# The row of a head's cumulative decays made by one full-height fp32r product in place of a 32-row f32 product

## Chip, core and metric

One NeuronCore of a Trainium2 chip runs the whole program. The metric is the device time of one execution in microseconds. Engines: PE is TensorE, PEld its weight loads, DVE is VectorE, ACT is ScalarE, POOL is GpSimd; SPq issues the DMAs.

## What is computed

The program is three layers on 256 tokens of width 1024: a first block (a mixer with a convolution branch and an SSM branch, then a mixture of 64 experts) and two layers of a second kind. The change lies in the SSM branch of the first block's mixer. Cut to that:

```
dt = softplus(n @ w_in[:, 7168:7200] + dt_bias)          # 32 heads, 256 tokens
ad = dt * a;  a_cs = cumsum(ad) within a chunk           # a = -exp(a_log)
seg[l, s] = a_cs[l] - a_cs[s];  L = exp(seg where s <= l)
y_diag = ((C B^T) * L) @ (x * dt)                         # for each head
```

The kernel works with chunks of 128 tokens (two of them) and carries the second chunk's share of the first through `rest`, the decay from each token of the first chunk to that chunk's end. To form `seg` for a head, the cumulative decays of that head, one row of 256 numbers, must stand on all 128 partitions.

## The kernel before

Weights stream from HBM into four slots of a ring (SyncE, `mixer_sp`, list `LOADS`), each slot refilled when the product four places back in the list is done. PE (`mixer_pe`) does first the projections: blocks of 8 accumulating products of 128x128 by 128x256 in f32 (`group`, line 176), then the 32-column product of `dt` (line 385), two "fillers" (blocks of the gate and z projection, also line 176), and the transposes of `dt`, `cs` and `rest` (line 171). An f32 product is two MATMUL instructions and two weight loads in the trace; an fp32r product is one of each.

DVE (`mixer_ve`) makes `dt` (lines 722, 724), `ex` = -dt*exp(a_log) (725), the two scans that give `cs` (728), `rest` (729), and then copies the five transposed pieces out as `col` (731).

The loop over heads, 34 steps on each of PE, DVE and ACT, is written out in a fixed order. On PE a step h holds, in this order: `decay(h)` (line 431, the product that the change replaces); a filler unless h % 4 is 3; in every fourth step pieces of the modulation rows (lines 333, 342); at h = 5, 13, 21 `prepare` of the next group of eight heads (417, 418 and eight transposes, 171); `mix(h-2)` (lines 443, 444), and behind the last odd heads of a group a sum of squares (201). On DVE a step holds `decay(h)` (three subtractions from the product's bank, 753 to 755), `weigh(h-1)` (759), a few taps of the convolution (700), `prepare` (737 to 745), `mix(h-2)` (765, 768) and, at h = 10, 18, 26, `norm` (reciprocal 218, then 777). On ACT: the exponential of step h (583), the copy of a filler (568 or 570), a square (194), and at h = 10, 18, 26 the square root (208), each change of function with a table load.

PE takes one of seven PSUM banks for each product and waits till the engine that last read that bank is done (`Ring.take`), so that nearly each product group begins with a wait:

```
b = ring.take(("cs", h))
if h == 0:
    e.wait_ge(*k.at("col", 1))
e.matmul(k.pb[b][:, 0:T], ident[0:32, h:h+1] broadcast to [32, 128], m_.cs, ...)
```

`mix(h)` on PE waits for `weigh(h)` on DVE. Behind the loop stand the remaining fillers, the convolution's mean and the mixer's tail (lines 488 to 490: fp32r products of values split into a rounded part and a remainder), then the experts, whose weights stream for about 950 us, then the two layers.

Of the kernel before, what the change touches and what calls it, by code (L numbers as in the profile page):

```python
# [7 lines left out]
F32 = mybir.dt.float32  # L8
# [3 lines left out]
ALU = mybir.AluOpType  # L12
ACT = mybir.ActivationFunctionType
# [3 lines left out]
T = 256  # L17
# [17 lines left out]
for _l in range(2):  # L35
# [3 lines left out]
CONST = [("ident", 128), ("ones", 128), ("amask", 128), ("lmask", 128), ("before", 128), ("iota", 256), ("upto", 64),  # L39
         ("kthr", 8), ("shift", 1), ("m64", 64), ("first", 1), ("cos", 32), ("sin", 32)]  # L40
ROWS = [("brt", 72), ("qhg0", 96), ("khg0", 96), ("qhg1", 96), ("khg1", 96)]
# [230 lines left out]
def mixer_sp(k, e):  # L272
# [4 lines left out]
    for n, (what, i) in enumerate(LOADS):  # L277
        if n >= 4:
            e.wait_ge(*mixer_used(k, *LOADS[n - 4]))
        c0 = {"ada": 512 * i, "a": 512 * i, "b": 1024 + 512 * i, "x": 4096 + 512 * i, "dt": 7168, "f": 2048 + 512 * i if i < 4 else 5152 + 512 * i}[what]  # L280
        wide = 32 if what == "dt" else 512
        w = a["w_ada"] if what == "ada" else w_in
        e.dma_start(k.slot(n % 4, [128, 8, wide]), w_tile(w, 0, 8, c0, c0 + wide)).then_inc(k.s(f"slot{n % 4}"), 16)
# [14 lines left out]
class Mix:  # L298


    def __init__(self, k):
# [6 lines left out]
        sm = k.tiles(89, 4)  # L308
        self.cs, self.dt, self.ex = sm[0:32, 0, :], sm[0:32, 1, :], sm[0:32, 2, :]
        self.rest = sm[0:32, 3, 0:128]  # L310
        self.ea = k.misc[0:32, 1:2]
        self.col = k.misc[:, 32:192]
# [34 lines left out]
def mixer_pe(k, e, emptied):  # L347
# [30 lines left out]
    for blk in range(6):  # L378
        w = mixer_slot(k, e, "x", blk, [128, 8, 512])
        for i in range(4):  # L380
            b, ins = product(("x", 4 * blk + i), w, 128 * i)
            ins.then_inc(k.s("mm_x"), 1)
            ring.until(b, *k.at("xt", 4 * blk + i + 1))
    b, ins = product(("dt", 0), mixer_slot(k, e, "dt", 0, [128, 8, 32]), 0, 32)
    ins.then_inc(k.s("mm_dt"), 1)
# [20 lines left out]
    e.wait_ge(*k.at("rest", 1))  # L406
    for i, x in enumerate((m_.dt[:, 0:128], m_.dt[:, 128:256], m_.cs[:, 0:128], m_.cs[:, 128:256], m_.rest)):
        ins = k.turn(e, k.pb[b][:, 32 * i:32 * i + 32], x, 32)
# [18 lines left out]
    def decay(h):  # L427
        b = ring.take(("cs", h))
        if h == 0:
            e.wait_ge(*k.at("col", 1))  # L430
        e.matmul(k.pb[b][:, 0:T], k.con("ident")[0:32, h:h + 1].to_broadcast([32, 128]), m_.cs, start=True, stop=True).then_inc(k.s("cs_row"), 1)
        ring.until(b, *k.at("decay", h + 1))
# [82 lines left out]
def mixer_ac(k, e, o):  # L515
# [39 lines left out]
    o.done(o.after().activation(m_.ex, m_.ex, ACT.Exp, scale=-1.0))  # L555
    o.done(o.after().activation(m_.ea, k.par("alog")[0:32, :], ACT.Exp))
    o.done(o.after().activation(m_.ex, m_.ex, ACT.Ln, bias=1.0), k.s("ln1p"))
# [105 lines left out]
def mixer_ve(k, e, o):  # L663
# [57 lines left out]
    e.wait_ge(*k.at("mm_dt", 1))  # L721
    o.done(o.after().tensor_scalar(dt, k.pb[k.bank["dt", 0]][0:32, 0:T], k.par("dtb")[0:32, :], None, ALU.add), k.s("dt"))
    e.wait_ge(*k.at("ln1p", 1))
    o.done(o.after().scalar_tensor_tensor(dt, dt, 0.0, ex, ALU.max, ALU.add))
    o.done(o.after().tensor_scalar(ex, dt, m_.ea, -1.0, ALU.mult, ALU.mult))
    for i in range(2):
        s = slice(128 * i, 128 * i + 128)
        o.done(o.after().tensor_tensor_scan(cs[:, s], k.con("ones")[0:32, :], ex[:, s], 0.0, ALU.mult, ALU.add))
    o.done(o.after().tensor_scalar(rest, cs[:, 0:128], -1.0, cs[:, 127:128], ALU.mult, ALU.add), k.s("rest"))
    e.wait_ge(*k.at("dt_turned", 1))  # L730
# [1751 lines left out]
def lay_out(i):  # L2482
# [5 lines left out]
            "sw": ij["ssm_conv_w"].reshape(4, 24, 128).transpose(2, 1, 0).reshape(128, 96), "sb": fm(ij["ssm_conv_b"]),  # L2488
            "dtb": ij["dt_bias"].reshape(32, 1), "alog": ij["a_log"].reshape(32, 1),
# [18 lines left out]
    for name, (at, width) in offsets(ROWS)[0].items():  # L2508
        line[0, at:at + width] = rows[name]
    out |= {"par": table, "rows": line, "const": constants(), "xT": np.ascontiguousarray(i["x"][0].T),  # L2510
            "w_rt": np.concatenate([ij["w_grp"], ij["w_er"]], axis=1)}
    for n in ("w_ada", "w_in", "w_cv_out", "w_ssm_out", "w_mix_out", "w1", "w3", "w2"):
        out[n] = ij[n]
# [6 lines left out]
def constants():  # L2520

    p = np.arange(128)
    q = p[None, :]
    p = p[:, None]
    pos = np.arange(T, dtype=np.float32)
    inv = np.float32(10000.0) ** (-np.arange(0, 32, 2, dtype=np.float32) / np.float32(32))
    ang = (pos[:, None] * inv[None, :]).astype(np.float32).reshape(2, 128, 16).transpose(1, 0, 2).reshape(128, 32)
    made = {"ident": p == q, "ones": np.ones((128, 128)), "amask": np.where(q <= p, 0.0, -3.0e38), "lmask": q >= p,
            "before": p < q, "iota": np.broadcast_to(np.arange(256), (128, 256)), "upto": (p <= q)[:, 0:64],
            "first": p % 32 == 0, "m64": q[:, 0:64] >= p % 64,  # L2530
            "kthr": np.arange(8) * BLKROWS + 65536.0 * ((p < NEAR) & (q[:, 0:8] == 0)), "shift": BLKROWS * (NEAR - (p < NEAR)), "cos": np.cos(ang), "sin": np.sin(ang)}
    return np.ascontiguousarray(np.concatenate([made[n] for n, _ in CONST], axis=1).astype(np.float32))
# [18 lines left out]
```

## Time and profile before

| what | us |
|---|---|
| median of 3 runs | 2592.53 |
| lowest and highest run | 2590.75, 2593.39 |
| span of the profiled execution | 2593.9 |
| projections of the mixer, up to the transposes of `dt` and `cs` | 41.1 to 191.5 |
| loop over heads | 193.65 to 371 |
| tail of the mixer | 390.5 to 490 |
| router and experts | 495 to about 1490 |
| PE, DVE, ACT busy | 2171.7, 1030.7, 677.7 |

The profiled execution is given by its span alone, 0.05% above the median of the runs. To read it: an engine's busy time says little by itself, since the stages are bound by different things; the chain of waits says which engine ended last at each time. A number behind "idle before" in a timeline row is how long the engine stood still, and the name is what it waited for; "issue" means that the profile shows nothing for it.

### The profile page before, as it was taken

To read this page: it belongs to the slowest core of one execution; us is meant where nothing else is said; L and a number is where in the kernel's file an instruction comes from. 1 tells how busy PE (TensorE), PEld (TensorE's weight loads), DVE (VectorE), ACT (ScalarE), POOL (GpSimd) and SP (SyncE) were. 2 spreads that over 40 slices of the span, in tenths; PEclk is the share of its full clock that TensorE was granted. 3 is DMA by queue.
4 is the path that set the end of the run, shared out by engine and by line. 5 is a ranking of instruction groups with operands and counts; after the bars stand their busy time and mean duration, and the time that the engine had idled before them with its cause. 6 is when DMAs were issued, how large, how long until landed. Compare 5 with 4: busy or idle time off the path is not lost.

```text
span 2593.9 us, 31929 instructions
## 1 busy us (share of the span) xinstructions
PE 2171.7 (84%) x13027; PEld 1588.3 (61%) x13027; DVE 1030.7 (40%) x2121; ACT 677.7 (26%) x1054; POOL 28.1 (1%) x47
## 2 busy tenths in 40 slices
PE   7999999876666666666667689979999999889999
PEld 4886679833322333233333266758899867668999
DVE  1577865510010010001010146772565257753653
ACT  2125665300000000000000122631554224623542
POOL 0000000000000000000000200000000200000000
PEclk8999999888888887888888899989999999999999
DMA  8443544599999999999999823214345424223442
GB/s 326 146 149 130 187 166 159 207 380 421 421 385 422 421 421 421 421 421 421 421 421 419 322 61 139 107 40 157 135 174 185 135 82 147 98 98 130 162 179 99
DMA packets 174501, 631.45 MB, mean 243 GB/s; under 512 B 10816, under 2 KB 28768, under 8 KB 125200
## 3 DMA queue, kind: packets, MB, share of 16 engines
q1 hardware_dynamic: 173008, 628.07, 61.8%
q0 software_dynamic: 1344, 1.28, 0.3%
q8 instruction: 106, 1.74, 0.3%
q14 instruction: 43, 0.35, 0.0%
HBM read 628.28 MB, written 1.05 MB: 243 GB/s over the span
## 4 chain that ended last, share of the span: by engine, by line
PE 57%; DMA 27%; DVE 10%; ACT 3%; SPq 2%; issue 1%; DVEq 0%; ACTq 0%
DMA ring<-in_w 26%; PE pb L176 23%; PE pb L1771 5%; PE pb L1772 5%; PE pb L1773 5%; PE pb L1055 4%; PE pb L1029 4%; SPq L942 2%; PE pb L1721 1%; PE pb L490 1%; PE pb L489 1%; PE pb L488 1%; DVE ar L2290 1%; PE pb L201 1%; DMA ring<-in_w_ada 1%
## 5 line engine op out<-in xcount | busy, mean ns | idle before, releaser
L176 PE MATMUL pb<-ar,ring 128*128 128x256 f32 (+1 forms) x2896 | 670.5, 391 | 49.8 <-ACT ar L1927 16.0
L176 PEld LDWEIGHTS pb<-ar,ring 128*128 128x128 f32 (+1 forms) x2896 | 554.8, 194 | 155.6 <-issue 54.7
L1029 PE MATMUL pb<-ring,ar 128*32 128x512 f32 x2048 | 277.0, 696 | 124.7 <-DMA ring<-in_w 124.1
L1771 PE MATMUL pb<-act,parts 128*128 128x256 f32 x1152 | 331.7, 288 | 12.1 <-DVE act L2375 12.1
L1772 PE MATMUL pb<-act,parts 128*128 128x256 f32 x1152 | 328.1, 285 | 0.0
L1773 PE MATMUL pb<-act,parts 128*128 128x256 f32 x1152 | 328.1, 285 | 0.0
L1055 PE MATMUL pb<-ring,ar 128*32 128x512 f32 x1024 | 172.1, 833 | 124.3 <-DMA ring<-in_w 124.3
L1029 PEld LDWEIGHTS pb<-ring,ar 128*32 128x32 f32 x2048 | 75.2, 125 | 306.0 <-issue 305.3
L1771 PEld LDWEIGHTS pb<-act,parts 128*128 128x128 f32 x1152 | 223.4, 194 | 13.3 <-issue 12.9
L1772 PEld LDWEIGHTS pb<-act,parts 128*128 128x128 f32 x1152 | 223.4, 194 | 0.4
L1773 PEld LDWEIGHTS pb<-act,parts 128*128 128x128 f32 x1152 | 223.2, 194 | 0.0
L1849 DVE TENSOR_TENSOR parts<-ring,parts 128x2048 fp32r<-128x2048 f32 x72 | 161.8, 2288 | 111.3 <-ACT parts L1842 111.3
L1055 PEld LDWEIGHTS pb<-ring,ar 128*32 128x32 f32 x1024 | 46.8, 146 | 237.5 <-issue 235.6
L1252 DVE TENSOR_TENSOR ar<-ar,pb 128x512 f32<-128x512 f32 x16 | 11.0, 688 | 425.4 <-PE pb L1029 425.4
L1106 ACT ACTIVATE ar<-pb 128x512 f32<-128x512 f32 x16 | 9.6, 597 | 599.6 <-PE pb L1055 599.6
L176 PE MATMUL pb<-ar 128*128 128x128 f32 x512 | 126.5, 421 | 44.7 <-DVE ar L1229 42.5
L176 PEld LDWEIGHTS pb<-ar 128*128 128x128 f32 x512 | 123.4, 335 | 59.0 <-DVE ar L1229 56.7
L1842 ACT ACTIVATE parts<-ring 128x2048 fp32r<-128x2048 f32 x72 | 133.5, 1901 | 79.0 <-PE pb L1773 76.3
L1260 DVE COPY ar<-pb 128x512 f32<-128x512 f32 x16 | 11.1, 692 | 285.7 <-PE pb L1055 285.7
L700 DVE SCALAR_TENSOR_TENSOR ar<-ar,par 128x256 f32<-128x256 f32 x240 | 104.7, 478 | 0.0
L1100 ACT ACTIVATE ar<-pb 128x512 f32<-128x512 f32 x16 | 9.6, 598 | 319.2 <-PE pb L1029 319.2
L488 PE MATMUL pb<-act,parts 128*128 128x256 f32 x256 | 73.7, 288 | 0.0
(367 smaller groups left out, 2416.3 us busy)
## 6 DMA issues: line engine op xcount, KB each, us to landing
ring<-in_w SPq DMA_DIRECT2D x384, 1024.0 KB, 18.7
ring<-in_w_in SPq DMA_DIRECT2D x36, 2048.0 KB, 7.8
ring<-in_w_ff SPq DMA_DIRECT2D x32, 2048.0 KB, 8.7
ring<-in_w_ada SPq DMA_DIRECT2D x12, 2048.0 KB, 12.1
ring<-in_w_ssm_out SPq DMA_DIRECT2D x4, 2048.0 KB, 8.2
ring<-in_w_out SPq DMA_DIRECT2D x4, 2048.0 KB, 7.9
ring<-in_w_cv_out SPq DMA_DIRECT2D x2, 2048.0 KB, 8.3
ring<-in_w_mix_out SPq DMA_DIRECT2D x2, 2048.0 KB, 7.7
```

The source lines that it names most:

```text
L176: ins = e.matmul(out, l, r, start=(i == 0), stop=(i == len(pairs) - 1))
L201: e.matmul(k.pb[SUMS][:, 0:T], k.con("ones"), k.tiles(85 + g % 2, 1)[:, 0, :], start=first, stop=last).then_inc(k.s("squared_sum"), 1)
L488: e.matmul(k.pb[b][:, 0:T], wh[:, j, c0:c0 + 128], xh[:, j, :], start=(j == 0), stop=False)
L700: made[m] = o.done(e.scalar_tensor_tensor(uc[:, m, :], ut[:, m, j:j + T], cw[:, m, j:j + 1], uc[:, m, :], ALU.mult, ALU.add), k.s("taps") ...
L942: e.dma_start(half_slot(k, n, [128, kt, 2048 // kt]), src).then_inc(k.s(f"expert{n % HALVES}"), 16)
L1029: ins = e.matmul(k.pb[b][32 * j:32 * j + 32, :], v.xg[i][:, kt, 32 * j:32 * j + 32], w[j][:, m, :], start=(kt == 0), stop=(kt == 7))
L1055: ins = e.matmul(k.pb[yb[c]][32 * j:32 * j + 32, :], v.ht[i][:, kt, 32 * j:32 * j + 32], w[j][:, m, 512 * c:512 * c + 512], start=(kt == 0 ...
L1771: e.matmul(k.pb[b][:, 0:T], wh[:, kt, c0:c0 + 128], xh, start=(first and kt == 0), stop=False)
L1772: e.matmul(k.pb[b][:, 0:T], wl[:, kt, c0:c0 + 128], xh, start=False, stop=False)
L1773: ins = e.matmul(k.pb[b][:, 0:T], wh[:, kt, c0:c0 + 128], xl, start=False, stop=(last and kt == 7))
L1842: o.done(o.e.activation(high[:, 4 * i:4 * i + 4, :], raw[:, 4 * i:4 * i + 4, :], ACT.Copy), k.s("ff_high"))
L1849: o.done(o.e.tensor_tensor(low[:, 4 * i:4 * i + 4, :], raw[:, 4 * i:4 * i + 4, :], high[:, 4 * i:4 * i + 4, :].bitcast(F32), ALU.subtract) ...
```

## The change

Each head's row of cumulative decays is spread over the partitions by one fp32r product over all 128 rows of the array in place of an f32 product over 32 rows.

- The `dt` projection has 128 columns in place of 32, from a new table `w_dt` that holds the 32 columns four times; `dt_bias` and `a_log` are repeated likewise. So `dt`, `ex` and `cs` stand on all partitions, four copies of the 32 heads.
- Four DVE instructions between `rest` and `col` make `cs_parts` (fp32r, 128x256: partitions 0 to 31 the value rounded by the conversion, 32 to 63 the remainder) and `pick_head` (fp32r, 128x32: the 32x32 identity on partitions 0 to 31 and again on 32 to 63, zero on the other 64).
- `decay(h)` on PE multiplies column h of `pick_head`, broadcast to 128 columns, with `cs_parts`; the first one waits for `cs_parts` in place of `col`.
- The table of constants is 32 columns wider.

```diff
-    c0 = {..., "dt": 7168, ...}[what]
-    wide = 32 if what == "dt" else 512
-    w = a["w_ada"] if what == "ada" else w_in
+    c0 = {..., "dt": 0, ...}[what]
+    wide = 128 if what == "dt" else 512
+    w = {"ada": a["w_ada"], "dt": a["w_dt"]}.get(what, w_in)
...
-        self.cs, self.dt, self.ex = sm[0:32, 0, :], sm[0:32, 1, :], sm[0:32, 2, :]
+        self.cs, self.dt, self.ex = sm[:, 0, :], sm[:, 1, :], sm[:, 2, :]
+        self.cs_parts, self.pick_head = k.parts[:, 3, 768:1024], k.parts[:, 3, 1024:1056]
...
-    b, ins = product(("dt", 0), mixer_slot(k, e, "dt", 0, [128, 8, 32]), 0, 32)
+    b, ins = product(("dt", 0), mixer_slot(k, e, "dt", 0, [128, 8, 128]), 0)
...
         if h == 0:
-            e.wait_ge(*k.at("col", 1))
-        e.matmul(k.pb[b][:, 0:T], k.con("ident")[0:32, h:h + 1].to_broadcast([32, 128]), m_.cs, start=True, stop=True).then_inc(k.s("cs_row"), 1)
+            e.wait_ge(*k.at("cs_parts", 1))
+        e.matmul(k.pb[b][:, 0:T], m_.pick_head[:, h:h + 1].to_broadcast([128, 128]), m_.cs_parts, start=True, stop=True).then_inc(k.s("cs_row"), 1)
...
-    o.done(o.after().tensor_scalar(dt, k.pb[k.bank["dt", 0]][0:32, 0:T], k.par("dtb")[0:32, :], None, ALU.add), k.s("dt"))
+    o.done(o.after().tensor_scalar(dt, k.pb[k.bank["dt", 0]][:, 0:T], k.par("dtb"), None, ALU.add), k.s("dt"))
...
-        o.done(o.after().tensor_tensor_scan(cs[:, s], k.con("ones")[0:32, :], ex[:, s], 0.0, ALU.mult, ALU.add))
-    o.done(o.after().tensor_scalar(rest, cs[:, 0:128], -1.0, cs[:, 127:128], ALU.mult, ALU.add), k.s("rest"))
+        o.done(o.after().tensor_tensor_scan(cs[:, s], k.con("ones"), ex[:, s], 0.0, ALU.mult, ALU.add))
+    o.done(o.after().tensor_scalar(rest, cs[0:32, 0:128], -1.0, cs[0:32, 127:128], ALU.mult, ALU.add), k.s("rest"))
+    o.done(e.memset(m_.pick_head[64:128, :].bitcast(F32), 0.0))
+    o.done(e.tensor_copy(m_.pick_head[0:64, :], k.con("id32")[0:64, :]))
+    t = o.done(e.tensor_copy(m_.cs_parts, cs))
+    o.done(o.after(t).tensor_tensor(m_.cs_parts[32:64, :], cs[32:64, :], m_.cs_parts[32:64, :].bitcast(F32), ALU.subtract), k.s("cs_parts"))
     e.wait_ge(*k.at("dt_turned", 1))
     o.done(o.after().tensor_copy(col, k.pb[k.bank["col", 0]][:, 0:160]), k.s("col"))
```

## Rows read from the trace of the kernel before

**Rows 1.** The page: span, and the chain that ended last by engine

```profile
span 2593.9 us, 31929 instructions
...
PE 57%; DMA 27%; DVE 10%; ACT 3%; SPq 2%; issue 1%; DVEq 0%; ACTq 0%
```

**Rows 2.** The chain of waits from 150 to 400 us, shares by line

```profile
by line: PE pb L176 52.7%; PE pb L431 6.1%; PE pb L443 5.3%; DVE ar L700 4.6%; PE pb L333 4.4%; PE pb L201 3.6%; PE pb L444 2.0%; PE pb L342 1.9%; DVE ring L745 1.4%; DVE ar L218 1.4%; issue 1.3%; DVE ar L777 1.3%; DVE ar L765 1.2%; DVE rin
```

**Rows 3.** Groups, 185 to 370 us: busy us, mean ns | idle before, releaser

```profile
L431 PE MATMUL pb<-ar,const 32*128 32x256 f32 x64 | 22.2, 426 | 2.3 <-DVE ar L765 2.3
...
L753 DVE TENSOR_SCALAR ring<-pb,misc 128x128 f32<-128x128 f32 x32 | 11.1, 347 | 20.1 <-PE pb L431 20.1
```

**Rows 4.** Timeline of PE, one decay product: start us, us, what

```profile
204.84 0.69 PE L431 MATMUL pb<-ar,const 32*128 32x256 f32 x2
205.47 3.72 PE L176 MATMUL pb<-ar,ring 128*128 128x256 f32 x16
```

**Rows 5.** Timeline at 390.5 us, the first fp32r products behind f32 ones

```profile
390.55 0.47 PE L488 MATMUL pb<-act,parts 128*128 128x256 f32 x1
390.74 0.19 PEld L489 LDWEIGHTS pb<-act,parts 128*128 128x128 f32 x1
390.86 0.28 PE L489 MATMUL pb<-act,parts 128*128 128x256 f32 x1
```

**Rows 6.** The page's groups: weight loads, f32 (L176) and fp32r (L1771)

```profile
L176 PEld LDWEIGHTS pb<-ar,ring 128*128 128x128 f32 (+1 forms) x2896 | 554.8, 194 | 155.6 <-issue 54.7
...
L1771 PEld LDWEIGHTS pb<-act,parts 128*128 128x128 f32 x1152 | 223.4, 194 | 13.3 <-issue 12.9
```

**Rows 7.** The chain of waits from 244 to 272 us: start us, us, what

```profile
245.67 0.58 PE pb L443 x2
...
246.50 0.48 DVE ar L765
...
248.14 0.42 ACT ar L194
...
253.99 1.75 DVE ar L218
...
258.81 0.47 DVE ring L759
...
269.89 0.40 DVE ar L765
```

**Rows 8.** Timeline, where PE waits in that stretch

```profile
259.37 0.62 PE L443 MATMUL pb<-ring 128*64 128x256 f32 x2 [0.46 <-issue]
...
270.33 0.69 PE L431 MATMUL pb<-ar,const 32*128 32x256 f32 x2 [0.78 <-DVE ar L765]
```

**Rows 9.** Timeline of DVE, waits for a decay product outside those stretches

```profile
276.13 0.35 DVE L753 TENSOR_SCALAR ring<-pb,misc 128x128 f32<-128x128 f32 x1 [1.50 <-PE pb L431]
...
350.39 0.35 DVE L753 TENSOR_SCALAR ring<-pb,misc 128x128 f32<-128x128 f32 x1 [0.49 <-PE pb L431]
```

**Rows 10.** Timeline around the place of the four new DVE instructions

```profile
192.04 0.33 DVE L731 COPY misc<-pb 128x160 f32<-128x160 f32 x1 [0.89 <-PE pb L171]
...
192.94 0.29 DVE L737 TENSOR_TENSOR ring<-pb,const 128x128 f32<-128x128 f32 x1 [0.58 <-PE pb L418]
...
193.65 0.69 PE L431 MATMUL pb<-ar,const 32*128 32x256 f32 x2
```

**Rows 11.** Groups of DVE with the nearest forms to the new instructions

```profile
L1277 DVE COPY ar<-ar 128x256 f32<-128x256 f32 x1 | 0.3, 285 | 0.0
L2096 DVE COPY misc<-pb 128x32 f32<-128x32 f32 x4 | 0.8, 192 | 19.0 <-PE pb L176 19.0
...
L768 DVE TENSOR_TENSOR ar<-ar 128x256 f32<-128x256 f32 x15 | 6.3, 420 | 0.3
```

**Rows 12.** Weight loads of line 176 by form, 172 to 184.6 us

```profile
L176 PEld LDWEIGHTS pb<-ar,ring 128*128 128x128 f32 x42 | 7.9, 190 | 1.4 <-issue 0.4
L176 PEld LDWEIGHTS pb<-ar,ring 128*32 128x32 f32 x16 | 1.7, 110 | 1.8 <-issue 0.3
```

**Rows 13.** Stages: us, PE busy (x), PEld, DVE, ACT, POOL, PEclk, DMA share, GB/s

```profile
247.02:270.33 23.31, 22.07 (x113) 15.47 (x112) 20.44 (x54) 14.14 (x18) 0.00 (x0) 1.00 0.45 164
...
495.00:502.40 7.40, 7.09 (x34) 7.12 (x35) 2.40 (x7) 3.73 (x8) 0.00 (x0) 0.50 1.01 421
```

**Rows 14.** Timeline of PE, the wait ahead of the router's products

```profile
495.31 1.10 PE L957 MATMUL pb<-ar 128*128 128x72 f32 x4 [3.50 <-ACT ar L1083]
```

More of the change, by code:

```diff
@@ L39 @@
 CONST = [("ident", 128), ("ones", 128), ("amask", 128), ("lmask", 128), ("before", 128), ("iota", 256), ("upto", 64),
-         ("kthr", 8), ("shift", 1), ("m64", 64), ("first", 1), ("cos", 32), ("sin", 32)]
+         ("kthr", 8), ("shift", 1), ("m64", 64), ("first", 1), ("id32", 32), ("cos", 32), ("sin", 32)]
 ROWS = [("brt", 72), ("qhg0", 96), ("khg0", 96), ("qhg1", 96), ("khg1", 96)]
@@ L279, in mixer_sp @@
             e.wait_ge(*mixer_used(k, *LOADS[n - 4]))
-        c0 = {"ada": 512 * i, "a": 512 * i, "b": 1024 + 512 * i, "x": 4096 + 512 * i, "dt": 7168, "f": 2048 + 512 * i if i < 4 else 5152 + 512 * i}[what]
-        wide = 32 if what == "dt" else 512
-        w = a["w_ada"] if what == "ada" else w_in
+        c0 = {"ada": 512 * i, "a": 512 * i, "b": 1024 + 512 * i, "x": 4096 + 512 * i, "dt": 0, "f": 2048 + 512 * i if i < 4 else 5152 + 512 * i}[what]
+        wide = 128 if what == "dt" else 512
+        w = {"ada": a["w_ada"], "dt": a["w_dt"]}.get(what, w_in)
         e.dma_start(k.slot(n % 4, [128, 8, wide]), w_tile(w, 0, 8, c0, c0 + wide)).then_inc(k.s(f"slot{n % 4}"), 16)
@@ L308, in __init__ @@
         sm = k.tiles(89, 4)
-        self.cs, self.dt, self.ex = sm[0:32, 0, :], sm[0:32, 1, :], sm[0:32, 2, :]
+        self.cs, self.dt, self.ex = sm[:, 0, :], sm[:, 1, :], sm[:, 2, :]
+        self.cs_parts, self.pick_head = k.parts[:, 3, 768:1024], k.parts[:, 3, 1024:1056]
         self.rest = sm[0:32, 3, 0:128]
-        self.ea = k.misc[0:32, 1:2]
+        self.ea = k.misc[:, 1:2]
         self.col = k.misc[:, 32:192]
@@ L406, in mixer_pe @@
     e.wait_ge(*k.at("rest", 1))
-    for i, x in enumerate((m_.dt[:, 0:128], m_.dt[:, 128:256], m_.cs[:, 0:128], m_.cs[:, 128:256], m_.rest)):
+    for i, x in enumerate((m_.dt[0:32, 0:128], m_.dt[0:32, 128:256], m_.cs[0:32, 0:128], m_.cs[0:32, 128:256], m_.rest)):
         ins = k.turn(e, k.pb[b][:, 32 * i:32 * i + 32], x, 32)
@@ L555, in mixer_ac @@
     o.done(o.after().activation(m_.ex, m_.ex, ACT.Exp, scale=-1.0))
-    o.done(o.after().activation(m_.ea, k.par("alog")[0:32, :], ACT.Exp))
+    o.done(o.after().activation(m_.ea, k.par("alog"), ACT.Exp))
     o.done(o.after().activation(m_.ex, m_.ex, ACT.Ln, bias=1.0), k.s("ln1p"))
@@ L2488, in lay_out @@
             "sw": ij["ssm_conv_w"].reshape(4, 24, 128).transpose(2, 1, 0).reshape(128, 96), "sb": fm(ij["ssm_conv_b"]),
-            "dtb": ij["dt_bias"].reshape(32, 1), "alog": ij["a_log"].reshape(32, 1),
+            "dtb": np.tile(ij["dt_bias"], 4).reshape(128, 1), "alog": np.tile(ij["a_log"], 4).reshape(128, 1),
             "dsk": fm(np.repeat(ij["d_skip"], 64)), "sng": fm(ij["ssm_norm_g"]), "n2g": fm(ij["norm2_g"]), "fg": fm(i["final_g"])}
@@ L2511, in lay_out @@
             "w_rt": np.concatenate([ij["w_grp"], ij["w_er"]], axis=1)}
+    out["w_dt"] = np.tile(ij["w_in"][:, 7168:7200], (1, 4))
     for n in ("w_ada", "w_in", "w_cv_out", "w_ssm_out", "w_mix_out", "w1", "w3", "w2"):
@@ L2529, in constants @@
             "before": p < q, "iota": np.broadcast_to(np.arange(256), (128, 256)), "upto": (p <= q)[:, 0:64],
-            "first": p % 32 == 0, "m64": q[:, 0:64] >= p % 64,
+            "first": p % 32 == 0, "id32": p % 32 == q[:, 0:32], "m64": q[:, 0:64] >= p % 64,
             "kthr": np.arange(8) * BLKROWS + 65536.0 * ((p < NEAR) & (q[:, 0:8] == 0)), "shift": BLKROWS * (NEAR - (p < NEAR)), "cos": np.cos(ang), "sin": np.sin(ang)}
```

## Prediction

> **What bounds the kernel.** I read the page first. Over the whole span PE ends last for 57% and DMA for 27% [rows 1], but the change touches one stage, the loop over heads and what leads to it, so the shares of the page settle nothing. The next view is the chain of waits from 150 to 400 us. There the line to look for is 431, the decay product: it holds 6.1% of that stretch [rows 2], 15 us, and nearly all the rest is PE too, with some DVE. So PE sets the pace and the 32 decay products lie in its queue. The groups of the same stage say how: 64 MATMULs, two for each head, and DVE's line 753 stood idle 20.1 us before its subtractions because it waited for line 431 [rows 3]. DVE is ahead of PE for most heads, and a sooner product is taken up at once.
>
> Not everywhere. In the finer chain, from 246.50 us the work that ends last leaves PE: it goes through DVE's line 765, ACT's 194 and the table loads, exponential, filler copy and square root behind it, DVE's reciprocal (218) and the norm's products, and comes to `weigh(10)` (759) at 258.81 and through DVE's own work to line 765 at 269.89 [rows 7]. PE meets it twice: `mix(10)` stands 0.46 us for `weigh(10)`, and the decay product of head 14 stands 0.78 us for the bank that line 765 gives back [rows 8]. The same picture comes again from 290.33 to 314.17 us, and the first half of it (to `mix(26)` at 347.04, again 0.46 us idle) from 334.16.
>
> **The part that gains: the decay product.** One costs 204.84 to 205.47, so 0.63 us from its start to that of the next block [rows 4]; I use 0.62, the least of these distances. After the change it is one MATMUL of 256 columns and one weight load. No row shows an fp32r product alone between two f32 blocks. The nearest is the first product of the mixer's tail behind f32 ones: from its start at 390.55 to that of the next at 390.86, 0.31 us [rows 5], and this pair also passes from f32 to fp32r. I take 0.31, so a head saves 0.31 us on PE. The bounds: in the stream behind it a product takes 0.12 us, from its load at 390.74 to its start at 390.86 [rows 5]; that saves 0.50. On the dear side a load that hides nothing and a product to its recorded end are 0.19 + 0.28 = 0.47 us [rows 5], which saves 0.15. The full height itself I price at nothing: every load of line 176 and 1771 has 128 rows, and these mean 194 ns in either type [rows 6]; loads lie inside the 0.31.
>
> The weight load of fp32r in this trace takes what the f32 load takes, 194 ns on both lines [rows 6]. The Trainium skill's page "TensorE: Matmul & The Clock Gate", section "Weight-path perf modes", says that the fast weight load goes on by itself when there are 128 weights and the input type is not FP32, and that about a factor of two is measured for it; by that rule, if fp32r counted as another type, the gain on PE would be near 8.6 us in place of 6.5. This trace doesn't agree.
>
> **How many heads count.** By the code's order, decay products 0 to 9 stand on PE before `mix(7)` hands over to DVE at 246.50: these 10 count. Products 10, 11 and 12 stand before `mix(10)` and 13 before the wait of product 14: the chain from 246.50 to 269.89 holds no PE work, so these 4 turn into longer waits of PE. Product 14 starts when DVE says, but its own length counts, with 15, 16 and 17: 4 more. The second group repeats it: 18 to 21 lost, 22 to 25 counted. In the third there is no `prepare`; 26, 27 and 28 are lost before `mix(26)`, and 29, 30 and 31 count. Together 10 + 4 + 4 + 3 = 21 heads count and 11 do not: 21 x 0.31 = 6.5 us.
>
> Would DVE follow? Where it waits for line 431 it stands 1.50 us at head 15 and 0.49 at head 29 [rows 9]; of the 12 such waits the one at head 2 is 0.46 and the others but these two are over 1.2. Between two of them at most two counted products lie, 0.62 us, and at heads 2 and 29 one, 0.31. So all of them keep some wait and the gain passes on.
>
> **The parts that cost.** (1) The four DVE instructions between `rest` and `col`. Nearest rows: copies of 128x32 at 0.19 and of 128x256 at 0.29, a two-input operation of 256 at 0.42 [rows 11]; the memset of 32 columns I take like the small copy, 0.19. Sum 1.1 us at most. The room there: DVE stands 0.89 us before line 731 and 0.58 before 737 [rows 10], 1.47 together, and line 737 waits for PE, not for DVE. So they are covered, with 0.4 to spare; if they were twice as long, 0.7 us would come through to DVE's first decay, which has idle time of its own before the second. PE's first decay product waits for `cs_parts`, due at about 192.3, and starts at 193.65 [rows 10]. Nothing. Bound: 0 to 0.7. (2) The `dt` product: its MATMULs stream 256 columns either way, its first load is 190 in place of 110 ns [rows 12], the others are hidden: +0.08 us on the path. (3) DVE's and ACT's work on `dt`, `ex` and `cs` goes by columns, not partitions (the 128-partition operation of 256 elements at 0.42 us [rows 11] is no longer than the same work on 32); nothing, at most a few hundredths. (4) The `dt` weights are 512 KB in place of 128 KB, issued four loads ahead, three blocks of four products of 3.72 us [rows 4] before they are needed; covered. The constants are 16 KB more ahead of the first weights, under 0.1 us even at half the 421 GB/s that a stage reaches [rows 13]; I take 0.04. (5) No step moves past another in any queue, and SyncE's list keeps its order. The tail's load of raw weights starts when PE's fillers are done and so moves along.
>
> **Sum.** -6.5 + 0.08 + 0.04 = -6.4 us. Behind the loop PE goes on without idle time worth naming into the fillers and the tail, and the experts' weights stream once PE and DVE hand over, so the gain should arrive at the end in full. The profiled execution would go from 2593.9 [rows 1] to 2587.5; its span lies 1.4 us above the median of the runs, and against that median, 2592.5, I forecast **2586.1 us**.
>
> **The rivals.**
> - *A hidden load.* By the cheap bound a head saves 0.50: 21 x 0.50 = 10.5, less 0.1, 2582.1 us. For it: the product's neighbours may hide its load. Against: nearly each group begins with a wait for a bank, and 0.62 is more than two passes. Chance 0.07.
> - *A load of half the length.* Half of 194 ns [rows 6] is 0.1 us, so a head would save 0.41: 21 x 0.41 = 8.6, less 0.1, 2584.0 us. Against: the 1152 loads of line 1771 show no such thing. The rule of the Trainium skill's page named above would work in this way. Chance 0.03.
> - *The others take it.* Once PE is 3.1 us ahead at head 10, ACT with its table loads or DVE could bind the PE-bound stretches too; then only the first ten heads give, 3.1 - 0.1 = 3.0, 2589.5 us. For it: DVE is busy 20.44 of 23.31 us in the second stretch [rows 13]. Against: the waits of [rows 9]. Chance 0.13.
> - *It gains nothing.* A single fp32r product between two waits might cost what two f32 passes do, because the fixed cost at a wait is what is paid: 2592.6 us. Against: of the 0.62 us the two passes themselves are 2 x 3.72 / 16 = 0.46 [rows 4], and only one, shorter, pass is left. Chance 0.08.
> - *Slower, by the clock.* PE will stand longer in three places: 0.46 + 3 x 0.31 = 1.4 us before `mix(10)`, `mix(18)` and `mix(26)`. Before the router's products PE stood 3.50 us, and these ran at a granted clock of 0.50, the lower of its two levels, 1.2 GHz, for the whole 7.40 us of the row; the loop ran at 1.00, with stops of 0.46 and 0.78 [rows 8, 13, 14]. If each of the three new stops brought such a stretch, it would cost 3.7 us each, 11.1 in all, and 2597.2 us would come out. It decides from 12.8 us at the lower clock in PE-bound work, which takes back the 6.4. Against: 1.4 is nearer 0.78 than 3.50. Chance 0.06.
>
> A difference of 0.2%, 5.2 us, is about what a measurement of this kernel can tell from none.
>
> **The numbers.** The forecast has 0.63; nearly all of it (0.59) lies beyond 5.2 us, and with the first two rivals that is 0.69 for faster. The third and fourth rivals and the rest of the forecast give 0.25 for no change, the clock 0.06 for slower. The range takes in the bounds: 21 x 0.50 gives 2582.1, and 21 x 0.15 less 0.1, and the third rival, give 2589.5; with half a microsecond for the runs, 2581.8 to 2590.0. It leaves out the last two rivals, 0.14.
>
> **What would show it.** Line 432 with 32 MATMULs in place of 64; its start to the next block's 0.31 us. PE's waits before the mix of heads 10, 18 and 26 near 1.4 us and before products 14 and 22 longer by 0.31. The loop ends (last mix product of head 31, at 370.5 before) 6.4 us sooner, and so does each later stage. DVE's line 736 starts at about 192.2, and 742 as before. I am wrong if the distance is under 0.2 or over 0.4 us, if the stretches 270 to 290 and 314 to 334 shrink by less than 1 us each, or if the gain at the end of the loop is not there at the end of the program.

## The result and the profile after

The changed kernel took 2586.36 us (median of 11 runs, 2583.44 to 2589.54); the kernel before, on the same chip, 2593.39. The two medians are 7.0 us apart. The ratio on record is 0.9967 with a 95% interval of 0.996 to 0.9975, which makes 8.6 us faster, between 6.5 and 10.4. The forecast was 2586.1 us. The profiled executions have spans of 2587.7 and 2593.9 [rows 1], 6.2 us apart. In what follows the line numbers of the changed kernel are the same up to line 308, one higher from there to line 730 and five higher from 735 on (731 to 734 are new): 431 became 432, 443 and 444 became 444 and 445, 753 became 758, 1055 became 1060.

The page has 32 instructions less on each of PE and PEld (13027 x2 before), and the chain of waits from 150 to 400 us gives the decay product 2.9% in place of 6.1% [rows 2]:

```profile
span 2587.7 us, 31869 instructions
PE 2159.1 (83%) x12995; PEld 1586.4 (61%) x12995; DVE 1031.7 (40%) x2125; ACT 677.2 (26%) x1054; POOL 28.1 (1%) x47
```

The groups of 185 to 370 us, to be held against [rows 3]:

```profile
L432 PE MATMUL pb<-parts 128*128 128x256 f32 x32 | 13.0, 406 | 2.4 <-DVE ar L770 2.4
L758 DVE TENSOR_SCALAR ring<-pb,misc 128x128 f32<-128x128 f32 x32 | 11.1, 348 | 12.4 <-PE pb L432 12.3
```

There are 32 products in place of 64, and DVE waits 12.3 us for them where it waited 20.1. The timeline of PE and of its weight loads shows one head, the same place as in [rows 4] but one head earlier (head 1):

```profile
201.26 0.38 PE L432 MATMUL pb<-parts 128*128 128x256 f32 x1
201.49 3.61 PE L176 MATMUL pb<-ar,ring 128*128 128x256 f32 x16
...
201.26 0.18 PEld L432 LDWEIGHTS pb<-parts 128*128 128x128 f32 x1 [0.84 <-issue]
201.37 3.33 PEld L176 LDWEIGHTS pb<-ar,ring 128*128 128x128 f32 x16
```

Before, the same head read like this:

```profile
199.78 0.69 PE L431 MATMUL pb<-ar,const 32*128 32x256 f32 x2
200.41 3.72 PE L176 MATMUL pb<-ar,ring 128*128 128x256 f32 x16
...
199.78 0.29 PEld L431 LDWEIGHTS pb<-ar,const 32*128 32x128 f32 x2 [0.84 <-issue]
200.40 3.32 PEld L176 LDWEIGHTS pb<-ar,ring 128*128 128x128 f32 x16 [0.33 <-issue]
```

The distance to the next block went from 0.63 to 0.23 us, not to 0.31, and the filler itself from 3.72 to 3.61. Over all heads the distance is now 0.20 to 0.30 us where a filler stands behind the product, and 0.31 or 0.40 where the mix does. Look at the loads: before, the filler's first load begins at 200.40, 0.62 us behind the start of the decay product, and the filler's first product starts with it; now it begins at 201.37, 0.11 us behind the decay product's own, and costs nothing.

By stretches of the loop, from the start of one decay product to that of another (h is the head; the last one ends at the first product of the tail, 390.55 before, 384.81 after):

| stretch | before | after | difference |
|---|---|---|---|
| h 0 to 10 | 53.37 | 48.11 | -5.26 |
| 10 to 14 | 23.31 | 24.58 | +1.27 |
| 14 to 18 | 20.52 | 18.21 | -2.31 |
| 18 to 22 | 23.32 | 23.58 | +0.26 |
| 22 to 26 | 20.51 | 18.21 | -2.30 |
| 26 to 29 | 14.97 | 16.89 | +1.92 |
| 29 to the tail | 40.90 | 39.57 | -1.33 |
| all | 196.90 | 189.15 | -7.75 |

The stretches in which the forecast counted a gain give 11.2 us, and those in which it counted none give back 3.45. The waits view of PE, 240 to 400 us, says where:

```profile
PE pb L444 <- issue: 6.5, 3, 2.2
PE pb L432 <- DVE ar L770: 1.7, 2, 1.0
```

PE stands 2.18 us before each of `mix(10)`, `mix(18)` and `mix(26)`, where it stood 0.46 [rows 8]. The view says "issue", but DVE's timeline shows what ends the first stop: `weigh(10)` ends at 256.30, 0.10 us before PE goes on.

```profile
255.75 0.55 DVE L764 TENSOR_TENSOR ring<-ring 128x384 f32<-128x384 f32 x1
```

The timeline of PE at the first two places:

```profile
256.40 1.08 PE L444 MATMUL pb<-ring 128*64 128x256 f32 x2 [2.18 <-issue]
...
257.84 2.83 PE L334 MATMUL pb<-ring,misc 128*32 128x512 f32 x16
260.60 0.38 PE L432 MATMUL pb<-parts 128*128 128x256 f32 x1
...
299.19 0.62 PE L444 MATMUL pb<-ring 128*64 128x256 f32 x2 [2.18 <-issue]
...
299.96 1.92 PE L334 MATMUL pb<-ring,misc 128*32 128x512 f32 x16
301.81 0.38 PE L432 MATMUL pb<-parts 128*128 128x256 f32 x1
```

and the windows view just behind each stop (us, PE, PEld, DVE, ACT, POOL busy, PEclk, DMA share, GB/s):

```profile
256.40:259.50 3.10, 3.10 (x12) 1.11 (x16) 3.10 (x10) 0.42 (x1) 0.00 (x0) 0.50 1.02 389
299.20:302.30 3.10, 3.10 (x23) 1.31 (x24) 3.10 (x10) 0.42 (x1) 0.00 (x0) 1.00 0.02 5
341.70:344.80 3.10, 3.10 (x18) 0.60 (x16) 2.03 (x6) 1.79 (x3) 0.00 (x0) 0.50 1.05 404
```

Behind the first and the third stop the granted clock is 0.50, the level of 1.2 GHz, and the same two products of the mix and eight of line 334 take 4.20 us (256.40 to 260.60) where they take 2.62 behind the second (299.19 to 301.81), 1.6 us more.

From the tail on the two profiles stay 5.7 us apart at the tail and at the router, 5.2 at the end of the experts and 6.2 at the end. The experts hold more than that shows; the end of the next section comes back to them.

### The profile page after: what moved, and what is told of

It reads as the page before. It is cut to its first block, busy times and chain, and to the rows that moved or that the text cites. A ratio compares the mean times of both kernels' runs of the same rounds, so it can differ in the third digit from the quotient of the medians.

```text
span 2587.7 us, 31869 instructions
## 1 busy us (share of the span) xinstructions
PE 2159.1 (83%) x12995; PEld 1586.4 (61%) x12995; DVE 1031.7 (40%) x2125; ACT 677.2 (26%) x1054; POOL 28.1 (1%) x47
## 3 DMA queue, kind: packets, MB, share of 16 engines
HBM read 628.68 MB, written 1.05 MB: 243 GB/s over the span
## 4 chain that ended last, share of the span: by engine, by line
PE 57%; DMA 27%; DVE 9%; ACT 3%; SPq 2%; issue 2%; DVEq 0%; ACTq 0%
DMA ring<-in_w 27%; PE pb L176 24%; PE pb L1776 5%; PE pb L1777 5%; PE pb L1778 5%; PE pb L1034 4%; PE pb L1060 4%; SPq L947 1%; PE pb L1726 1%; PE pb L489 1%; PE pb L490 1%; PE pb L491 1%; PE pb L201 1%; DVE ar L2295 1%; DMA ring<-in_w_ada 1%
## 5 line engine op out<-in xcount | busy, mean ns | idle before, releaser
L176 PE MATMUL pb<-ar,ring 128*128 128x256 f32 x2896 | 668.2, 391 | 49.8 <-ACT ar L1932 16.0
L176 PEld LDWEIGHTS pb<-ar,ring 128*128 128x128 f32 x2896 | 557.7, 195 | 145.2 <-issue 46.3
L176 PE MATMUL pb<-ar 128*128 128x128 f32 x512 | 126.5, 423 | 44.8 <-DVE ar L1234 42.5
L176 PEld LDWEIGHTS pb<-ar 128*128 128x128 f32 x512 | 123.5, 336 | 59.1 <-DVE ar L1234 56.7
L1265 DVE COPY ar<-pb 128x512 f32<-128x512 f32 x16 | 11.1, 692 | 285.7 <-PE pb L1060 285.7
```

Source lines behind the costliest of these rows:

```text
L176: ins = e.matmul(out, l, r, start=(i == 0), stop=(i == len(pairs) - 1))
```

## The experiments

Two theories stood at first. **Shape:** a head pays for changes of the weights' shape on PE. 32 rows and 128 rows (or 64 columns and 128) can't be loaded ahead of one another, so some 0.2 us of load is exposed at each change; full height takes two such changes away, fp32r takes one pass away. **Wait** (the forecast's): the wait for a bank exposes a load in any case, the height is worth nothing, and only fp32r counts.

**1. `e1_f32_full_height`**: the wide `dt` and `cs`, but the decay product in f32 over all 128 rows, with a column of the 128x128 identity.

```diff
-        e.matmul(..., m_.pick_head[:, h:h + 1].to_broadcast([128, 128]), m_.cs_parts, ...)
+        e.matmul(..., k.con("ident")[:, h:h + 1].to_broadcast([128, 128]), m_.cs, ...)
```

> The changed kernel with the decay product in f32 over all 128 rows of the array (column h of the full identity by cs, which stands on 128 partitions), so two passes as before but the full height of the change. Theory S (a group's first weight load is exposed only where the shape of the weights changes, 32 rows to 128 rows): from a decay product to the end of the filler block behind it (head 4) 4.28 us before, 3.77 after; here about 4.08, since two passes stay (0.32 more) but the exposed load goes (0.2 less). Theory W (the one of the prediction: the wait for a bank exposes the load, height is nothing): 4.28, as before. Time by S: about 21 x 0.2 = 4 us under the kernel before less what is given back in the DVE-bound stretches; by W: as before.

**2. `e2_fp32r_64_rows`**: fp32r, but only over the 64 rows that hold the two parts.

```diff
+        e.matmul(..., m_.pick_head[0:64, h:h + 1].to_broadcast([64, 128]), m_.cs_parts[0:64, :], ...)
```

> The changed kernel with the fp32r product over 64 rows only (the rounded value and the remainder, without the 64 rows of zeros); same result. Theory S: 64-row weights between 128-row ones expose a load at both sides, so decay to the end of the filler about 3.96 us (0.31 + 3.65), 0.2 more than the change's 3.77, and about 3 to 4 us slower than the change. Theory W: the load is exposed in either case, no difference from the change. A third, T (the type fp32r lets the next load go ahead): 3.77 as in the change.

**3. `e3_wide_dt_only`**: everything wide, but the decay product as before, f32 over 32 rows.

```diff
+        e.matmul(..., k.con("ident")[0:32, h:h + 1].to_broadcast([32, 128]), m_.cs[0:32, :], ...)
```

> All of the change but the product itself: dt over 128 columns, cs on 128 partitions, the four new DVE instructions, the wider constants; the decay product again f32 over 32 rows. By the prediction's steps it costs 0.08 + 0.04 us: the time of before within 0.1%, the transposes of dt and cs (PE line 171) 0.1 us later than their neighbours explain, the first decay product not waiting. The rival (the additions cost something real, since the changed kernel's loop began 2.0 us later than before in its profile): 1 to 2 us slower than before, in each profile.

The timelines of PE at a decay product with a filler behind it (head 1), of the first and the second of these:

```profile
199.08 0.70 PE L432 MATMUL pb<-ar,const 128*128 128x256 f32 x2
199.61 3.62 PE L176 MATMUL pb<-ar,ring 128*128 128x256 f32 x16
```

```profile
200.01 0.38 PE L432 MATMUL pb<-parts 64*128 64x256 f32 x1
200.31 3.72 PE L176 MATMUL pb<-ar,ring 128*128 128x256 f32 x16
```

In the table both distances run from the start of the decay product of head 4, the first to the start of its filler, the second to the start of the block behind the filler. (The recorded end of the filler, which the expectations speak of, lies 0.07 us later in each kernel.)

| kernel | to the filler | to the block behind the filler | loop | ratio of the times |
|---|---|---|---|---|
| before | 0.62 | 4.28 | 196.90 | 1 |
| full height, f32 | 0.53 | 4.08 | 193.03 | 1.0005 (0.9996 to 1.0014) |
| 64 rows, fp32r | 0.31 | 3.96 | 190.28 | 0.9984 (0.9975 to 0.9993) |
| wide, 32 rows, f32 | 0.62 | 4.27 | 196.85 | 1.001 (1.0 to 1.0019) |
| full height, fp32r | 0.22 | 3.77 | 189.15 | 0.9967 (0.996 to 0.9975) |

The second distance settles it. Height alone is worth 0.20 (4.28 to 4.08, in f32) and 0.19 (3.96 to 3.77, in fp32r); fp32r alone is worth 0.32 (4.28 to 3.96) and 0.31 (4.08 to 3.77). The two add up and don't depend on each other. By the code a wait for a bank stands ahead of the filler in all five, so such a wait doesn't expose the load; the change of shape does. And 64 rows cost what 32 cost, in spite of fp32r: the filler's first load begins 0.31 us behind the decay product's start with 64 rows and 0.11 us with 128.

The heads without a filler are the counter-check. Behind the decay product of head 3 stands the mix, with weights of 64 columns, so the shape changes there whatever the height. From this product to that of head 4 is 1.42 us before and 1.42 at full height in f32, 1.10 over 64 rows and 1.11 over 128 rows in fp32r: there the height is worth nothing. So the 0.2 us of the table is the price of one change, the one behind the product. Where line 201, with weights of 128 by 128, stands in front of the decay product, the change in front is gone too: from head 10 to head 11, with such a block ahead of both products, it is 0.39 us less at full height in f32 (6.13 to 5.74).

With 64 rows the distance is 0.31 us, as in the forecast, and the loop is 6.62 us shorter, near the forecast's own 21 x 0.31 = 6.5. Over the stretches that count it is 0.31 us for each of the 21 heads, so the count of heads was sound. That the 64-row product has the forecast's distance is a coincidence: the forecast took it from a product of 128 rows. The Trainium skill, page "TensorE: Matmul & The Clock Gate", section "Step-by-step: what each phase is for", says that PE pulls a weight load ahead of running products where row groups don't conflict or where it goes to the background buffer. The rows agree for loads of one shape (the filler's load at 0.11 us). Where the shape changes they don't show it: the load begins 0.31 us behind the product's start.

The times are another matter. Full height in f32 shortens the loop by 3.87 us and the time not at all, and the wide `dt` alone makes the time 0 to 0.19% longer with the loop unchanged. Both were run again.

**4. `e11_f32_full_again` and `e12_wide_dt_again`**: the first and the third kernel again, in more runs.

> e1 again in more rounds. Its profile had the loop 3.9 us shorter than before, its time did not (1.0005, 0.9996 to 1.0014). If the loop's gain reaches the end, the ratio is about 0.9985; if the parts beside the product cost something real, as e3's ratio of 1.001 hints, it is near 1.000 again.

> e3 again in more rounds. If the parts beside the product cost 0.1 us, as the prediction has it, 1.0000 within 0.0005; if they cost what e3's middle value says, 1.001 again (2.6 us), with no stage of the loop longer than before.

The ratios were 1.0 (0.9991 to 1.0009) and 1.0009 (1.0 to 1.0018): both hold. The cause lies outside the loop, among the experts; see below.

**5. `e4_after_more_fillers`**: the change, with a filler also in steps 11, 19 and 27, so that PE has 3.6 us of work in the stops before `mix(10)`, `mix(18)` and `mix(26)`. The fillers are taken from behind the loop.

```diff
-    return h % 4 != 3
+    return h % 4 != 3 or h in (11, 19, 27)
```

> The changed kernel with three of the fillers that PE does behind the loop done in steps 11, 19 and 27, which have none, ahead of the place where PE stands 2.18 us for weigh(10), (18), (26), and where in two of three cases the clock fell to half for 3.4 us. Theory 1 (the stops and the low clock that follows take back part of the gain): stops of 2.18 us go to under 0.5, no low clock in the loop, and the end of the loop comes nearer by 3 x 2.2 plus about 3 us for the two dips, so 5 to 9 us under the changed kernel. Theory 2 (ACT's copy of one more filler with its table load puts the chain through ACT and DVE back): the chain from mix(7) to weigh(10) grows and the gain is under 2 us.

2580.23 us, ratio 0.9947 (0.9934 to 0.9961), 6 us under the change by the medians and 5 by the ratios. The loop went from 189.15 to 181.88. The stops before the mixes are gone, no stretch of the loop is below a granted clock of 1.00, and one new stop stands in the waits view of PE, before the tail, because the loop now has the fillers that stood there:

```profile
PE pb L489 <- DVE act L805: 2.9, 1, 2.9
PE pb L432 <- DVE ar L770: 1.4, 2, 0.7
```

```profile
376.22 0.48 PE L489 MATMUL pb<-act,parts 128*128 128x256 f32 x1 [2.85 <-DVE act L805]
376.50 0.42 PE L490 MATMUL pb<-act,parts 128*128 128x256 f32 x1
```

The products behind it take 0.21 us each up to 379.7 and 0.12 from there; from the start of the tail to the router is 106.2 us in place of 104.8.

**6. `e10_after_two_fillers`**: only the fillers at 11 and 19, to leave PE some work before the tail.

> As e4, but with fillers in steps 11 and 19 only; the third stays behind the loop, where e4 had a new stop of 2.85 us before the tail's first product and the lower clock behind it. Theory: the stop of 2.18 us before mix(26) is back, the one before the tail is gone or under 0.5 us; the tail starts 0.7 us sooner than in e4, with up to 1.6 us more or less by where a dip falls: between 2577.5 and 2581, the same as e4 within its interval. The rival (each filler in the loop is worth what e4 gained by three, 6 us over 3): 2 us slower than e4.

2580.73 us, ratio 0.9944 (0.9931 to 0.9958). The new stop is gone, one of 2.2 us before `mix(26)` is left. The loop is 180.91, the tail 104.8, and the time can't be told from that of the version with three fillers.

**7. `b_e7_before_more_fillers`**: the same three fillers on the kernel before. If they only filled PE's stops, they should be worth little here, where the stops are 0.46 us.

> The kernel before with the three fillers moved to steps 11, 19 and 27, as in e4. PE stands only 0.46 us at each of the three places before, so if the stops are what e4 removed, the gain here is 3 x 0.46 = 1.4 us (0.05%), against 6 us on top of the change. If it gains 5 us or more, the fillers' place pays for another reason (work taken out of the part behind the loop).

2598.53 us, ratio 1.0009 (1.0 to 1.0018): no gain, and the loop 2.1 us longer. The expected 1.4 us can't be seen alone, because the new stop of experiment 5 stands here too: 2.86 us before the tail, with a granted clock of 0.50 behind it from 393.96 to 397.37.

```profile
392.88 0.36 PE L488 MATMUL pb<-act,parts 128*128 128x256 f32 x1 [2.86 <-DVE act L800]
```

With three fillers the change has this stop as well, and gains all the same. So the fillers pay because the change made PE wait. Two fillers on the kernel before, which would leave the new stop out, were not tried.

**8. `b_e5_before_again` and `e9_after_again`**: the kernel before and the change, profiled once more, to see what varies between executions.

> The kernel before once more, profiled beside the others of this set. The expert stage (router's first product to the end of the experts' last product) was 982.7 us in its first profile with blocks of four experts 59.6 to 60.0 apart, and 59.85 to 60.0 apart in all of the changed programs. Theory P (the programs stream their weights at slightly different rates, by where the tables lie in memory): 982.7 again, steps of 59.6. Theory N (the rate differs from run to run or chip to chip): up to 4 us more, steps near 59.9.

> The changed kernel once more, for its profile. In the first one PE stood 2.18 us before mix(10), mix(18) and mix(26), and behind the first and the third the clock was at half for 3.4 us, 1.6 us each. If the dips belong to the kernel, at least one of the three stops shows one again and the stretch from the first decay product to the first product of the tail is near 189 us; if they were chance of that run, there is none and the stretch is about 186.0 us.

The loop was 196.89 and 188.57 us. From the router to line 1075 the kernel before took 982.6 us in both of its profiles, so the experts' stretch hardly varies between executions of one kernel. In the second profile of the change the three stops are 2.18 us again, and the clock falls behind the first and the second this time, not the third:

```profile
256.40:259.50 3.10, 3.10 (x12) 1.08 (x16) 3.10 (x10) 0.42 (x1) 0.00 (x0) 0.50 1.04 403
...
300.70:303.80 3.10, 3.10 (x15) 1.09 (x8) 3.10 (x10) 1.63 (x3) 0.00 (x0) 0.50 0.00 0
...
341.10:344.50 3.40, 2.50 (x20) 0.88 (x20) 3.30 (x11) 1.01 (x3) 0.00 (x0) 1.00 0.97 336
```

So it isn't a matter of the place alone, and not of DMA beside it either: the low clock stands beside a DMA share of 0.00 and the full clock beside 0.97.

**9. `b_e6_before_with_table`**: the kernel before with the input `w_dt`, which nothing reads, in case the experts run otherwise because arrays lie elsewhere in HBM. **`e8_fillers_dt_in_place`**: experiment 5 without `w_dt`; four DMAs write the same 32 columns of `w_in` side by side.

```diff
...
+            for r in range(4):
+                e.dma_start(dst[:, :, 32 * r:32 * r + 32], w_tile(w, 0, 8, c0, c0 + 32)).then_inc(...)
...
```

> The kernel before with the 512 KB table w_dt among its inputs, read by nobody: no instruction changes, only where the tables behind it lie in memory. Theory P (the place of the tables costs what e3 showed, 0.1% to 0.19%): 2.6 to 4.9 us slower than before. Theory N: no difference within 0.1%.

> e4 without the table w_dt: the 32 columns of dt are fetched four times from w_in by four DMAs into the four column blocks of the slot, so that the large tables lie where they lay before. Theory P: 2.6 to 4.9 us under e4, near 2576 to 2577.5 us. Theory N: the same as e4 within 1 us. If the 4096 short packets were late, PE line 176 would wait for them ahead of the dt product.

The ratios were 1.0004 (0.9995 to 1.0014), and 0.9948 (0.9934 to 0.9962) against 0.9947 with the table. The theory of the table fell: it is neutral in both kernels.

**Where full height in f32 lost its gain.** The 14 profiles together show where. Between router and second layer two things differ, and each goes with a property of the kernel and not with the execution.

First, the rate at which the experts' weights come. The view of the DMA queues from 780 to 960 us, of before, of before with the table, of the change and of the change with `dt` in place, in this order:

```profile
DMA packets 10408, 75.83 MB, mean 421 GB/s; under 512 B 1157, under 2 KB 1157, under 8 KB 1157
```

```profile
DMA packets 10399, 75.82 MB, mean 421 GB/s; under 512 B 1150, under 2 KB 1150, under 8 KB 1150
```

```profile
DMA packets 10355, 75.50 MB, mean 419 GB/s; under 512 B 1145, under 2 KB 1145, under 8 KB 1145
```

```profile
DMA packets 10370, 75.51 MB, mean 420 GB/s; under 512 B 1158, under 2 KB 1158, under 8 KB 1158
```

The engines are full (DMA share 1.01) and PE waits for them, so 0.4% less in 180 us is 0.4% more time. From the first group of line 1055 to the last, fifteen steps, is 904.5 to 905.4 us in the four profiles of kernels with the old table of constants and 907.7 to 909.5 in the ten with the new one; the shortest single step is 59.58 in the four and 59.84 or 59.85 in all ten. The means are 904.9 and 908.6: **3.7 us lost** in the mean by every kernel that has the change's wide `dt` and its 32 extra columns of constants, whatever its decay product. The table `w_dt` isn't the cause, since before with it is among the four and the change without it among the ten. What is common to the ten is that buffers in SBUF lie elsewhere and that `dt` is wide; which of these it is was not tried.

Second, the products behind the last expert, line 1002 (1007). The timelines of before, and of the change:

```profile
1471.22 5.17 PE L1002 MATMUL pb<-ar 128*128 128x256 f32 x16 [2.87 <-issue]
```

```profile
1467.53 3.69 PE L1007 MATMUL pb<-ar 128*128 128x256 f32 x16 [0.90 <-DVE ar L1265]
```

and of the wide `dt` alone, second run:

```profile
1472.32 5.41 PE L1007 MATMUL pb<-ar 128*128 128x256 f32 x16 [2.18 <-issue]
```

Before, PE stands 2.87 us for nothing that the profile names, and the 16 products run at a mean granted clock of 0.71; in the change they start as soon as DVE has freed the bank, at 1.00. The windows view of these products, before and in the change:

```profile
1471.22:1476.30 5.08, 5.08 (x16) 4.01 (x16) 0.00 (x0) 0.00 (x0) 0.00 (x0) 0.71 1.05 395
```

```profile
1467.53:1471.10 3.57, 3.57 (x16) 2.93 (x16) 0.00 (x0) 1.26 (x2) 0.00 (x0) 1.00 0.90 299
```

From the last group of line 1055 to the next layer's sums (line 1075) is 25.2 to 25.7 us in the eight profiles of kernels whose decay product is f32 (13027 MATMULs and as many loads) and 21.1 to 22.6 in the six with fp32r (12995): **3.8 us gained** in the mean by every kernel with these 64 instructions fewer on PE. That such a stop comes and goes with the number of instructions ahead of it, a thousand microseconds after them, fits the loading of PE's code in blocks, a boundary of which lies at this place or not. The page of either kernel lists a DMA queue of kind "instruction" with 106 packets:

```profile
q8 instruction: 106, 1.74, 0.3%
```

They are of 16 KB each, and one of them falls here in all 14 traces. In the eight with the stop PE goes on 2.3 to 3.0 us after this packet began. In the six without it PE goes on from 0.5 us before the packet to 1.1 us behind it, so there it doesn't wait for it. This supports the reading; but the trace doesn't tie the packet to PE, and the view gives "issue" and no more, so the cause is argued, not shown.

With the two the ratios add up within their intervals, all but that of the 64-row kernel. The mean loop of the two profiles of the change is 188.9, 8.0 under before; +3.7 and -3.8 cancel; 8.6 was measured. Full height in f32: -3.9 + 3.7, measured +1.3 and 0. The wide `dt` alone: +3.7, measured +2.6 and +2.3. Fp32r over 64 rows: -6.6 + 3.7 - 3.8 = -6.7 by the loop and the means, and -4.1 (1.8 to 6.5) was measured, so about 2.5 us of this one stay open. With three fillers: -15.0 + 3.7 - 3.8 + 1.4 = -13.7, measured -13.7, and -13.5 without the table. With two: -16.0 + 3.7 - 3.8 = -16.1, measured -14.5 (10.9 to 17.9 less). The fillers on the kernel before: +2.1 + 1.4 = +3.5, measured +2.3. What is behind line 1075 takes 1112.6 to 1116.3 us, with no order by kernel, so a single profile can be off by some microseconds at its end.

## Why the prediction was right, and where not

The time, 2586.1 against 2586.36, is better than its working. The forecast's gain of 6.4 us lies just under the measured 6.5 to 10.4, and it started from a median of 2592.5 where the eleven runs gave 2593.39. Above all, errors of 4.6 and 3.45 us and two effects of nearly 4 us that it knew nothing of cancelled one another in large part, and that was luck. What it had right was which engine sets the pace, which heads count and where the rest is lost. Step by step:

- **What bounds the kernel** held. PE bound the loop but for the stretches behind a `norm`. DVE still waited for decay products at 11 places, before at 12, 12.3 us in all for 20.1, and the rival that the others take the gain fell: heads 14 to 17 and 22 to 25 give 2.31 and 2.30 us.
- **A head's gain** is the step that failed: "the full height itself I price at nothing", and 0.31 us a head. It was 0.53 over the first ten (5.26 us). With a filler behind it (head 4) it was 0.51, of which 0.32 is the second pass and 0.19 the height. Of that 0.19 half lies in the distance to the filler (0.22 us in place of 0.31) and half inside the filler, where the forecast didn't look. The row taken as nearest, the first product of the tail [rows 5], is followed by one of the same shape, 128 by 128, and shows nothing of what a change of shape costs the block behind. What [rows 4] could have said is that the 3.72 us of the filler behind a decay product are 0.1 more than the 3.62 of a filler behind a product of its own shape. In before's own trace line 201, two f32 passes over 128 rows, passes to a filler in 0.54 us (361.99 to 362.53), and the 32-row product in 0.63. The rival of the hidden load (0.50 a head, chance 0.07) named the right size. It spoke of the decay product's own load; what is hidden now is the load of the block behind it.
- **A load of half the length** fell: the loads of line 432 have a mean of 187 ns, near the 194 ns of f32 and fp32r loads in [rows 6].
- **How many heads count** held: 21 heads at 0.53 are 11.1 us, and the stretches that count gave 11.2. The 64-row kernel, 6.62 against 21 x 0.31, is the cleaner proof, since its stretches that don't count changed by 0.02 us at most.
- **The stops** before the three mixes were put at 1.4 us and are 2.18: the same sum with 0.5 to 0.6 a head for 0.31. "1.4 nearer 0.78 than 3.50" was right for 1.4; the 64-row kernel has just these stops (1.4 us) and full height in f32 stops of 1.2, and neither has a lower clock behind them. At 2.18 it came behind two of three, in both profiles. **The clock rival**, chance 0.06, came true in part. Two stretches at 0.50 took 1.6 us more each in their products, in place of the 3.7 put down for each of three. In the loop it is less where a wait for a bank follows: h 18 to 22 took 23.58 us at the full clock and 24.63 in the second profile with the lower one, 1.05 more; h 26 to 29 took 16.89 with the lower clock and 15.25 without, 1.64 more. So the two cost some 2.7 us in the first profile and 2.1 in the second.
- **The four DVE instructions** took 0.09, 0.17, 0.28 and 0.42 us, 0.94 with their gaps (193.64 to 194.58), against 1.1 allowed. They are covered, as forecast: from the transposes to the first decay product is 2.14 us before, 2.11 with the wide `dt` alone and 1.94 in the change. The timeline of DVE:

```profile
193.64 0.09 DVE L731 MEMSET parts<- 64x32 f32 x1
193.75 0.17 DVE L732 CAST parts<-const 64x32 fp32r<-64x32 f32 x1
193.85 0.28 DVE L733 CAST parts<-ar 128x256 fp32r<-128x256 f32 x1
194.16 0.42 DVE L734 TENSOR_TENSOR parts<-ar,parts 32x256 fp32r<-32x256 f32 x1
194.68 0.33 DVE L736 COPY misc<-pb 128x160 f32<-128x160 f32 x1
```

  Line 736 began 0.96 us behind the transposes (0.53 before), its wait having shrunk; the forecast's clock time of 192.2 was missed by 2.5 us, 2.2 of it because the whole stage began later.
- **The `dt` product**, priced at +0.08, had the wrong sign. With 128 columns two changes of shape are gone. From the first projection product to the transposes is 150.1 to 150.2 us in four profiles of kernels with the wide `dt` and 150.4 to 150.5 in two of before, all with the full clock from 3 us behind that first product. Where the clock rose 6 us behind it, it is 151.7 to 151.8 in four and 152.0 in one of before. So it is worth about 0.25 us; that this is the mechanism of the heads is likely and was not tried by itself.
- **The start** varies: the first projection product stood at 41.08 us before and 39.58 in the second profile of it, at 41.96 in the change. Of the 2.0 us by which the loop began later in its profile, 0.9 are this, and 1.3 are the clock that rose 6 us behind that product in place of 3, less what the `dt` product gains. The start varied between executions of the kernel before too, and the late clock was there in one profile of its kind and in four of those with the wide `dt`.
- **Behind the loop** the gain should "arrive at the end in full". Tail to router it did (104.76 in both). Through the experts it did too, but by two effects of nearly 4 us and opposite sign that the forecast knew nothing of: it had set "the constants are 16 KB more" and the wider `dt` at 0.04 and 0.08 us, and gave the number of instructions no price at all. Had only one of them come, the change would have stood near 2582.6 or 2590.1.

From the forecast's -6.4 to what was measured: the heads -4.6 (11.1 for 6.5); the three stretches priced at nothing +3.45, some 2.7 of it the clock; `dt` -0.3; the two effects among the experts -0.1. That makes -7.95, and -8.6 (-10.4 to -6.5) was measured.

## To carry to other kernels

Before costing a small product between large ones, look at what its weights' shape does to its neighbours: hold the distance from its start to the **end** of the block behind it against a place where the shapes are the same; here weights of 32 or 64 rows ahead of a block of 128 cost it about 0.2 us, in f32 and in fp32r alike. Where a change makes the bounding engine faster, list where it will wait next, and move independent work there: here that was worth 5 to 6 us, more than half of what the change gave, and on the kernel before it gave no gain. And where a change of a few microseconds doesn't add up, compare far stages over several profiles by the build: a layout or an instruction count can be worth as much there as the edit is where it was made.

## What the runs showed of the hardware

- A weight load began 0.11 us behind the start of an fp32r product of the same weight shape, with the code's wait for a bank between them, and 0.31 us behind it where the rows went from 64 to 128. The change of rows behind a decay product cost 0.20 us in f32 (4.28 to 4.08) and 0.19 in fp32r (3.96 to 3.77). Where the block behind has 64 columns, so that the shape changes in any case, full height was worth nothing (1.42 and 1.42 us; 1.10 and 1.11).
- A stop of PE of 2.18 us was followed by a granted clock of 0.50 four times in seven (twice in each profile of the change, not in that with two fillers), and the same ten products then took 4.20 us in place of 2.62. Stops of 1.2 and 1.4 us were not followed by it, and stops of 2.85 or 2.86 us before the tail were, three times in three.
- DMA at full rate gave 421 or 422 GB/s in the four profiles of kernels with the old table of constants and 419 or 420 in the ten of kernels with this table 128 bytes wider on each partition and `dt` four times as wide, 3.7 us over the experts.
- A stop in PE's queue of 2.05 to 3.42 us, put down to "issue", was there in eight profiles, each time ended 2.3 to 3.0 us after a 16 KB packet of the instruction queue began, and was gone in the six of kernels with 64 instructions fewer on PE.
